# A decoder layer's prologue rearranged: bias copies, parameter rows, sample key products, low weight parts, the split of x

## The reference, cut to what matters

```
proj = x @ w_in                      # 3072 columns: conv gates and input, q, k, v
conv = B * conv3(C * h)              # 4 groups of 64 channels
attn = dilated window attention, 12 heads of 64, shared relative-position bias
       (prompt: 256 keys of its own; sample: 256 cached keys each, plus its own key)
x = LN(alpha*x + [conv, attn] @ w_out)
x = LN(alpha*x + memory attention (4 heads, 256 tokens))
x = LN(alpha*x + top-4-of-32 experts, clamped SwiGLU)
outputs also: new k and v rows, conv state, memory k and v
```

## Time and profile before

| | us |
|---|---|
| median of 3 executions | 1408.44 (1399.79 to 1411.55) |
| the profiled execution | 1414.02 |
| its span, first to last instruction | 1412.1 |
| TensorE busy | 1224.5 (87%) |
| VectorE busy | 376.2 (27%) |

### The profile page before, as it was taken

One profiled execution on the slowest core, in us unless ns is written; L12 is line 12 of the kernel. 1 busy time (PEld: TensorE's weight loads), 2 busy tenths in 40 slices (PEclk: granted clock), 3 DMA queues, 4 the chain that ended last, 5 costly groups with the idle time before them and its releaser, 6 DMA issues.

```text
span 1412.1 us, 16873 instructions
## 1 busy us (share of the span) xinstructions
PE 1224.5 (87%) x6509; PEld 617.4 (44%) x6509; DVE 376.2 (27%) x843; ACT 210.1 (15%) x370; POOL 78.8 (6%) x61
## 2 busy tenths in 40 slices
PE   3896997995887999999899998999889898898986
PEld 2894443874674334333433343333433333333332
DVE  3365433117325221202212032021220202212023
ACT  3441222022312010010110101101001010100001
POOL 2014300004001000000000000000000000000001
PEclk7998999998997999999999999999999999999999
DMA  9885799515991999999999999999999999999993
GB/s 289 178 255 164 181 164 337 179 65 201 364 417 74 364 418 416 416 419 417 419 418 416 417 419 417 419 417 416 418 419 418 419 417 416 418 418 418 417 416 130
DMA packets 104709, 487.17 MB, mean 345 GB/s; under 512 B 8948, under 2 KB 10636, under 8 KB 71296
## 3 DMA queue, kind: packets, MB, share of 16 engines
q1 hardware_dynamic: 99296, 469.47, 85.3%
q0 software_dynamic: 3824, 15.62, 4.2%
q10 hardware_dynamic: 1552, 1.57, 0.4%
HBM read 479.40 MB, written 7.24 MB: 345 GB/s over the span
## 4 chain that ended last, share of the span: by engine, by line
PE 56%; SPq 24%; DVE 9%; issue 4%; ACT 3%; DMA 3%; POOL 1%; DVEq 0%; POOLq 0%
PE ps L1730 19%; SPq L569 13%; SPq L565 11%; PE ps L1433 11%; PE ps L1752 10%; PE ps L1464 4%; PE ps L1762 3%; PE ps L1702 2%; DMA ring<-in_w_gate_up_dram 2%; PE ps L1583 1%; DVE arena L1350 1%; DVE ring L1064 1%; ACT arena L917 1%; PE ps L1418 1%; DMA arena<-in_b_gate_up_dram 1%
## 5 line engine op out<-in xcount | busy, mean ns | idle before, releaser
L1730 PE MATMUL ps<-ring,arena 128*64 128x512 f32 x1536 | 340.1, 594 | 11.7 <-DMA ring<-in_w_gate_up_dram 11.7
L1333 DVE TENSOR_SCALAR arena<-ps 128x512 f32<-128x512 f32 x32 | 22.2, 693 | 703.0 <-PE ps L1730 703.0
L1730 PEld LDWEIGHTS ps<-ring,arena 128*64 128x64 f32 x1536 | 108.8, 137 | 228.1 <-issue 188.4
L1752 PE MATMUL ps<-ring,arena 128*64 128x512 f32 x768 | 170.1, 596 | 22.6 <-ACT arena L917 22.6
L1762 PE MATMUL ps<-arena 128*128 128x264 f32 x256 | 92.4, 507 | 34.5 <-DVE arena L1350 33.6
L1752 PEld LDWEIGHTS ps<-ring,arena 128*64 128x64 f32 x768 | 53.1, 137 | 124.2 <-issue 95.9
L911 ACT ACTIVATE arena<-arena 128x512 f32<-128x512 f32 x32 | 20.2, 632 | 578.3 <-DVE arena L1333 578.3
L1433 PE MATMUL ps<-arena,ring 128*128 128x264 f32 x384 | 89.2, 395 | 5.1 <-DVE arena L1120 3.7
L1464 PE MATMUL ps<-x_split,w_split 128*128 128x264 f32 x576 | 75.0, 294 | 21.1 <-DVE w_split L949 21.1
L1762 PEld LDWEIGHTS ps<-arena 128*128 128x128 f32 x256 | 52.2, 239 | 80.5 <-DVE arena L1350 62.6
L1730 PE MATMUL ps<-late,arena 128*64 128x512 f32 x384 | 85.3, 593 | 0.3 <-DMA late<-in_w_gate_up_dram 0.3
(11 more groups left out here) (264 smaller groups left out, 990.6 us busy)
## 6 DMA issues: line engine op xcount, KB each, us to landing
ring<-in_w_gate_up_dram SPq DMA_DIRECT2D x192, 1024.0 KB, 20.5
ring<-in_w_down_dram SPq DMA_DIRECT2D x96, 1024.0 KB, 24.4
late<-in_w_gate_up_dram SPq DMA_DIRECT2D x48, 1024.0 KB, 19.3
late<-in_w_down_dram SPq DMA_DIRECT2D x24, 1024.0 KB, 23.4
arena<-in_w_gate_up_dram SPq DMA_DIRECT2D x16, 1024.0 KB, 19.2
ring<-in_w_in_dram SPq DMA_DIRECT2D x12, 1024.0 KB, 22.2
ring<-in_cache_mem_k_dram SPq DMA_DIRECT2D x8, 1024.0 KB, 4.9
ring<-in_cache_mem_v_dram SPq DMA_DIRECT2D x8, 1024.0 KB, 8.1
```

Of the source, the lines that this page charges most:

```text
L1333: nc.vector.tensor_scalar(g2, ps[:, 0, :], 7.0, None, ALU.min).then_inc(e_g2, 1)
L1730: ins = mm(ps[64 * j:64 * j + 64, gu, :], x, w[:, D * gu + 512 * j:D * gu + 512 * j + 512], start=(c < 0), stop=(c == 7), skip_group_check ...
L1752: ins = mm(ps[64 * j:64 * j + 64, 4 + half, :], x, w[:, kk, 512 * half:512 * half + 512], start=(m == 0), stop=(m == 7), skip_group_check= ...
```

## The change

- **Order of loads.** The memory tokens come behind the first four pieces of `w_in`.
- **x.** Each of the eight chunks gets a PSUM bank of its own. ScalarE only casts (`x_hi` from PSUM); VectorE copies `xT` from PSUM and subtracts `x_lo` from PSUM.
- **Low weight parts.** `w_lo` is written over the piece of `w_in` in the ring slot itself (`ring_split`, the same memory as float32r). So a slot is free when TensorE has used the piece, and no longer when VectorE has subtracted it; `w_lo` waits for no buffer.
- **Small work moved.** The bias matmuls and small turns (`small_turns`) run after `win_half(1)`, the memory's turns (`turn_memory`) after `win_half(3)`. The three casts of `b_gate_up` by ScalarE come after the first, second and third group of tiles (before: one ahead of the first weight piece, then after the first and second group). The convolution is spread over more pieces.
- **Parameters.** `w_conv` and the layer norms' scales and shifts are loaded as rows (38 rows of 512 B) and turned once by TensorE; before, 4-byte elements were loaded to columns.
- **Bias.** 16 copies of the row go to DRAM, and not 128; GpSimd reads the diagonals back with 16 DMAs (8 blocks of 16 partitions, two groups of heads) as soon as the copies have landed.
- **Token rows.** They use banks 4, 6, 0, 2, 4, 6; ScalarE copies three of the six, VectorE three. The sample's own scores (`own_scores`) move from ahead of the head loop into its step 1.
- **Sample key products.** VectorE makes them (`key_products`, in steps 2 to 9 ahead of `key_sums`); GpSimd only issues the four spread loads, and then the stores.

```diff
-    s = [("xp", 0), ("mp", 0)] + [("win", i) for i in range(12)]
+    s = [("xp", 0)] + [("win", i) for i in range(4)] + [("mp", 0)] + [("win", i) for i in range(4, 12)]
...
             elif what == "win":
-                eng.wait_ge(s_wlo, 2 * i + 2)
+                piece_used(eng, 2 * i + 1)
...
-            pool.dma_start(scratch_bias, b_row[0:H, :].unsqueeze(1).broadcast_to((H, P, 384))).then_inc(s_bscr, 16)
+            pool.dma_start(scratch_bias, b_row[0:H, :].unsqueeze(1).broadcast_to((H, SHIFTS, 384))).then_inc(
+                s_bscr, 16)
+            pool.wait_ge(s_bscr, 16)
+            for j in range(P // SHIFTS):
+                for i, (h0, h1) in enumerate(((0, SPLIT_HEADS), (SPLIT_HEADS, H))):
+                    diagonals = bass.AP(scratch_bias.tensor, P - 1 - SHIFTS * j + SHIFTS * 384 * h0,
+                                        [[383, SHIFTS], [SHIFTS * 384, h1 - h0], [1, 256]])
+                    pool.dma_start(bias_parts[i][SHIFTS * j:SHIFTS * j + SHIFTS], diagonals).then_inc(s_bias, 16)
...
-            for b in range(NS):
-                if b % 2 == 0:
-                    spread("qb", scratch_q, AW, b // 2, s_spread)
-                products("qb", "wk", AW, b)
+            for i in range(NS // 2):
+                spread("qb", scratch_q, AW, i, s_spread[i])
...
-                nc.scalar.copy(xT[:, c, :], ps[:, c % 4, 0:T]).then_inc(s_xT_out, 1)
-                act.wait_ge(s_xT_out, c + 1)
-                nc.scalar.copy(x_hi[c], xT[:, c, :]).then_inc(s_xhi, 1)
-            act.wait_ge(s_bgu, 48)
-            nc.scalar.copy(bgu3[0:2 * NX, :], bgu_f[0:2 * NX, :]).then_inc(s_bcut, 1)
+                nc.scalar.copy(x_hi[c], ps[:, c, 0:T]).then_inc(s_xhi, 1)
...
+                nc.vector.tensor_copy(xT[:, c, :], ps[:, c, 0:T]).then_inc(s_xT_out, 1)
+                nc.vector.tensor_tensor(x_lo[c], ps[:, c, 0:T], x_hi[c].bitcast(F32), ALU.subtract).then_inc(s_xlo, 1)
+            low_parts(0, 4)
             dve.wait_ge(s_bt, 1)
...
+            def key_products(b):
+                arrived(dve, ("qb", b // 2))
+                arrived(dve, ("wk", b))
+                q = slot(("qb", b // 2))[:, (b % 2) * AW:(b % 2 + 1) * AW]
+                k = halves(("wk", b))[:, :, 0:AW]
+                nc.vector.tensor_tensor(k, k, q.unsqueeze(1).broadcast_to((P, 2, AW)), ALU.mult).then_inc(s_kq, 1)
...
+                if step == 1:
+                    own_scores()
                 if 2 <= step < 2 + NS:
+                    key_products(step - 2)
                     key_sums("wk", AW, H, step - 2, step - 1, s_kr)
...
             for i in range(6):
                 win_half(i)
+                if i == 1:
+                    small_turns()
+                if i == 3:
+                    turn_memory()
```

More of the change, by code:

```diff
@@ L232, in decoder_layer, with bias_of @@
         pt = view(a_pt, 2, 512)
-        assert top[0] == ARENA + LATE
+        a_tail = region(3 * D)
+        assert top[0] == ARENA + LATE and a_tail <= ARENA + EARLY
+        bias_parts = (view(a_mix + 4 * T, SPLIT_HEADS, 256), view(ARENA + EARLY, H - SPLIT_HEADS, 256))
+        def bias_of(h):
+            return bias_parts[0][:, h, :] if h < SPLIT_HEADS else bias_parts[1][:, h - SPLIT_HEADS, :]
         x_hi, x_lo = ([x_split[:, i, c, :] for c in range(DC)] for i in range(2))
-        w_hi, w_lo = ([w_split[:, b, i, :] for b in range(2)] for i in range(2))
-        bgu_f = view(a_mix, 2 * D)
+        w_hi = [w_split[:, b, :] for b in range(2)]
+        bgu_f = view(a_proj + K0 * T, 2 * D)
         b_row = view(a_xh + D, 384)
[L239 to L242, removed]
+        es = view(a_tail, 264)
+        pts = view(a_tail + 264, 2, 128)
+        selfw = view(a_tail + 264 + 256, 128)
+        avs = view(a_tail + 264 + 384, 2, D)
         stT = tiny(2 * 16).rearrange("p (c n) -> p c n", c=2)
@@ L245, in decoder_layer @@
         ul = tiny(2 * 2).rearrange("p (c k) -> p c k", c=2)
-        wc = tiny(6).rearrange("p (k c) -> p k c", k=3)
-        gcol = [tiny(DC) for _ in range(2)]
-        bcol = [tiny(DC) for _ in range(2)]
+        par = tiny(6 + 4 * DC)
+        wc = par[:, 0:6].rearrange("p (k c) -> p k c", k=3)
+        gcol, bcol = ([par[:, 6 + DC * (2 * i + j):6 + DC * (2 * i + j) + DC] for i in range(2)] for j in range(2))
+        par_rows = view(a_xh + D + 384, P)
         mx, nm, sm, rs = (tiny(4).rearrange("p (a b) -> p a b", a=2) for _ in range(4))
@@ L295, in decoder_layer @@
         assert 804 + T <= 2 * AW
-        extra = [view(a, 2048) for a in (a_memT, a_memv, a_lg, a_bias + D)]
-        yo = view(a_bias, 3, D)
+        extra = [view(a, 2048) for a in (a_memT, a_memv, a_lg, a_tail + D)]
+        yo = view(a_tail, 3, D)
         landed = [sem(f"landed{s}") for s in range(RING)]
@@ L342, in decoder_layer @@
         s_yz = sem("s_yz")
-        s_spread = sem("s_spread")
+        s_spread = [sem(f"s_spread{i}") for i in range(4)]
         s_conv = sem("s_conv")
@@ L429, in arrived @@
                 if key[0] == "qb":
-                    eng.wait_ge(s_spread, 16 * (key[1] + 1))
+                    eng.wait_ge(s_spread[key[1]], 16)
                 else:
@@ L639, in _ @@
                                   tab[0:NX + 1, :].unsqueeze(1).broadcast_to((NX + 1, NS, H))).then_inc(s_zero, 1)
[L640 to L645, removed]
+            pool.dma_start(par_rows[0:6, :], w_conv[0].rearrange("k (c p) -> (k c) p", p=P)).then_inc(s_par, 16)
+            for i, v in enumerate((ln1_g, ln1_b, ln2_g, ln2_b)):
+                pool.dma_start(par_rows[6 + DC * i:6 + DC * i + DC, :], v[0].rearrange("(c p) -> c p", p=P)).then_inc(
+                    s_par, 16)
+            with nc.allow_non_contiguous_dma(reason="one router bias per row"):
                 pool.dma_start(brc[0:NX, :], b_router[0].rearrange("(e a) -> e a", a=1)).then_inc(s_par, 16)
@@ new lines, in small_turns @@
+            def small_turns():
+                pe.wait_ge(s_const, 48)
+                pe.wait_ge(s_zero, 2)
+                oh = con("oh")[0:NX + 1, :]
+                tb = tab[0:NX + 1, :]
+                mm(ps[0:H, 4, 0:384], tb, oh[:, 0:384], start=True, stop=True)
+                for c in range(2):
+                    mm(ps[:, 5, c * H:(c + 1) * H], oh[:, 384 + c * P:384 + (c + 1) * P], tb, start=True, stop=True)
+                mm(ps[0:NS * H, 5, 32:33], tab8[0:NX + 1, :], oh[:, 640:641], start=True, stop=True)
+                for c in range(2):
+                    tp(ps[:, 6, 16 * c:16 * c + 16], xh[0:2 * NS, 0, P * c:P * c + P], ident[0:2 * NS, 0:2 * NS])
+                pe.wait_ge(s_par, 16 * 6)
+                n_par = 6 + 4 * DC
+                tp(ps[:, 6, 32:32 + n_par], par_rows[0:n_par, :], ident[0:n_par, 0:n_par]).then_inc(s_bt, 1)
```

169 lines of the change are left out of this document (85 added, 84 removed).

## The result

The changed kernel takes 1413.73 us (median of 20 runs, 1407.55 to 1423.26), the kernel before 1405.93 (20 runs beside it, 1395.61 to 1412.57): ratio 1.0059, 95% interval 1.0037 to 1.0082. It is slower, by 0.6%, where I had forecast 1394 and 1380 to 1405. Its profiled execution took 1410.73, span 1408.9. That pair of profiles misleads: the one of before took 1414.0, 8 above the median of its kernel, the one of after 3 less than its median.

What follows compares the result with a forecast made beforehand. Bound by a prologue until the first expert frees slots, then a DMA-rate load stream. Terms -16.4, +1.6, -8.9, +3.1, +6 sum to -14.6 from profiled 1414.0: 1399.4; median 5.6 lower, so 1394, range 1380 to 1405.

Steps and rivals of the forecast that it cites:

- What goes through the DMA queues in the loop: Head loop: earlier GpSimd stores and later SyncE loads share the queues; TensorE waits some 6 us, range 0 to 14.
- rival B: Head loop: slow DMA stretch also catches step 5's load, landing 27 us after issue; 1403 to 1405 us, chance 0.12.
- Start of the w_in products: Prologue: first `w_in` product starts at 17.2 us instead of 33.67, -16.4 us.
- What moves into the products: During the `w_in` products: small and memory turns added there, some old waits gone; +1.6 us, range 0 to +6.
- The ring: Weight slots freed 3 to 6 us later; loads behind them needed after 100 us, so no cost before the head loop.
- Bias and parameters: Prologue DMA: smaller bias write and its reading back stay hidden, freed bandwidth is worth nothing; 0 us.
- End of the products to the first probabilities: Between `w_in` products and first head: shorter copies, own scores moved, faster scalings, less slow clock; -8.9 us, range -6 to -11.
- The head loop: Key products on VectorE lengthen three uncovered TensorE waits to 2.9 us; +3.1 us, up to 6 more by the clock.

Runs made afterwards that it cites:

- run 9: Changed kernel with key products and sums only in head-loop steps covered by a half of the memory products, element stores left in place: 1396.28 us, ratio 0.9935.
- run 10: Changed kernel with key products and sums only in covered head-loop steps, and the four element stores replaced in place by whole-row stores: 1381.60 us, ratio 0.983.
- run 12: Kernel before without the four element stores, that part of the output left out: 1407.91 us, ratio 1.001.
- run 5: Changed kernel without the four element stores, that part of the output left out: 1395.21 us, ratio 0.9926.
- run 7: Changed kernel with element stores moved behind the memory key store and ScalarE's first `b_gate_up` cast back ahead of the weights: 1410.30 us, ratio 1.0027.
- run 11: Changed kernel with element stores moved behind the memory key store and 128 shifted bias copies again instead of 16: 1399.07 us, ratio 0.9951.
- run 1: Changed kernel with the four element stores moved behind the memory key store, after the sample attention: 1401.59 us, ratio 0.9966.
- run 2: Changed kernel with all eight stores of that block, large ones too, moved behind the sample attention: 1401.90 us, ratio 0.9956.
- run 6: Changed kernel with element stores moved behind the memory key store, and key products and sums only in covered head-loop steps: 1388.91 us, ratio 0.9871.
- run 3: Kernel before with the four element stores moved behind the memory key store: 1404.88 us, ratio 0.9987.

## Why the prediction was wrong

The step that failed is *What goes through the DMA queues in the loop*. Its term was +6, within 0 to 14; in its place the runs show 18.5 us (the changed kernel with and without the element stores, 1413.7 and 1395.2), and 12.1 when they are only moved. I had the parties right: the elements, GpSimd's early arrival, SyncE's late loads, a rate of 10 to 50 GB/s. The order was wrong. I counted the last `w_mem_v` as queued ahead of the elements, arriving in time, and let only `w_mem_k` fall into the low stretch. Counted, as the prediction does, from the scores of step 3 (127.64 in the profile after), the load was to share the queues from +5; it was issued at +8.4, and the first element store at +6.9. My own rows gave the price of being caught: 26.9 us from issue to landing, measured now at 27.99. The wait is 16.72 us, and the half behind it runs in part at the lower clock (8.84 against 7.13). The half at 135.96 (9.22) stands ahead of that wait, behind the one of 2.97 for VectorE. That is the mechanism of rival B ("the hole takes both"), to which I gave 0.12 and the reason "the load is queued before the elements start"; that reason was false. Its time, 1403 to 1405, was some 9 us too low, because less had been won elsewhere than I summed, as the table below shows.

The Trainium skill's rule of turns between queues, packet by packet (DMA: Bandwidth & Descriptors, Queues, rings and completion order), would, with the even share of bytes that I read into it, have made this term about 0. The runs decide against the even share: runs 9 and 10 store the same bytes around the same load, and it lands after 25.9 us in one and 10.0 in the other. Whether the turns by packet hold, no run here shows. Another rule of the same page bears on that pair (Rules for kernel authors): a transfer whose last dimension isn't contiguous becomes one descriptor per element, and should be rearranged. The runs agree that it should be rearranged here, 14.7 us between the two.

The other steps, from the profiles of run 12 and run 5. Both leave out the element stores, so the low stretch that they cause is in neither. Each is a single execution, 2.7 and 4.3 us above its median. TensorE's first start of each stage, us:

| stage begins | run 12 (before) | run 5 (changed) | difference | forecast |
|---|---|---|---|---|
| first turn of probabilities | 132.6 | 110.7 | -21.9 | -23.7 |
| sample attention | 232.9 | 217.6 | -15.3 | -20.6 |
| `w_out` products | 247.3 | 236.8 | -10.5 | -20.6 |
| first layer norm | 279.4 | 268.9 | -10.5 | -20.6 |
| first gate and up products, streamed | 456.9 | 446.3 | -10.6 | -20.6 |

- *Start of the w_in products*, -16.4: right. 16.45 against the 17.2 said; run 7 showed that it passes to the end.
- *What moves into the products*, +1.6, and *The ring*, 0: right. The wait behind piece 3 is 2.13, `w_in` ends at 100 (101 said).
- *Bias and parameters*, 0: right for the bias copies (run 11); the parameters as rows were not run by themselves.
- *End of the products to the first probabilities*, -8.9: right within 1 to 2 us; with the two steps above -21.9 of -23.7.
- *The head loop*, +3.1 and up to +9: the mechanism is right, the term too small. The three waits are 2.97, 2.93 and 2.93, as said (2.9). The stage got longer by 6.6 in the table (run 5 against run 12): 3.0 are the waits for VectorE, 1.0 is a wait for `w_mem_v` that is left without the stores, and 2.5 are the same products taking longer (TensorE busy 92.7 us in place of 90.1), the clock, which I had let be the same in both.
- Not in the prediction at all: the sample attention. It takes 14.4 us in run 12 and 19.2 in run 5, with the same products and the same short waits ahead of them. The changed order alone doesn't bring this: runs 1 and 7, which have it, took 14.4 us, the changed kernel 16.0 and run 2 19.2. The first window of that stage, of run 12 and then of run 5, shows only another clock:

```profile
233.00:239.00 6.00, 6.00 (x64) 1.49 (x64) 0.00 (x0) 0.80 (x1) 0.00 (x0) 1.00 0.06 5
```

```profile
218.00:224.00 6.00, 6.00 (x40) 1.14 (x32) 0.00 (x0) 0.00 (x0) 0.00 (x0) 0.53 0.00 0
```

- The rest passes whole: -10.5 at `w_out`, -10.6 at the experts, and the medians differ by 1407.9 - 1395.2 = 12.7. That is 7.9 us less than the 20.6 forecast for these steps together; with the 12.5 us by which the 18.5 exceed the 6, it makes up the miss of 19.7.

So against before: 12.7 us won, 18.5 lost to the elements, 5.8 slower by this sum and 7.8 measured. The forecast had -20.6 and +6.

Not settled: what VectorE waits for where the trace names no releaser in its core (3.30 us in run 1; none in run 5, without the stores). Moved stores seem to cost something still in the changed order: run 5 is 6.4 us below run 1, and run 10 is 7.3 below run 6, but the intervals overlap in both pairs. And a single profile places such differences badly. From the first layer norm to the first expert the profiles took 168.5 (run 3), 168.6 (the changed kernel), 172.3 (run 5) and 181.3 us (run 2), at mean granted clocks of 0.93, 0.93, 0.91 and 0.87, while from the first expert to the end all fourteen profiles (before, after and the twelve runs) took 956.6 to 958.7.

## What to carry to other kernels

Taking work off an engine moves everything behind it in its list forward. Before such an edit, write down what is behind it (here eight stores, four of them of 2560 elements in all), and what other list is released at the same moment; then ask which load would be caught. What a store of elements costs depends on what stands beside it (nothing in the old order, 18.5 us in the new) and not on its few bytes: turn it into rows (two small transposes and a copy here; from the last `w_in` product to the first turn of probabilities run 10 takes 10.1 us and run 6 takes 9.7) wherever a load that somebody waits for can stand beside it, and only then take the gain of the earlier start. And a step of work that fits under a covering block is to be placed by that block, not by its turn: that alone was worth 12.7 us with the element stores moved (run 6 against 1) and 17.5 with them in place (run 9 against the changed kernel).

## What was not expected of the hardware

- 10 KB written as 4-byte elements hold the DMA engines at a share above 1 and 22 to 81 GB/s for about 12 us, and everything queued with them (a 1 MB load 25.2 to 28.0 us, a 0.4 KB write 22 to 25 us) lands after. The same bytes as 1 KB rows leave no such stretch: the load lands in 10.0 and the small write in 7.9.
- The granted clock differs between stages that the trace shows alike: the same products after the same waits of 1.3 and 0.7 us ran at 1.00 in run 12 and at 0.53 in run 5 (whole stage: 14.4 us in runs 1, 7 and 12, 19.2 in runs 2 and 5). TensorE was busy all through both windows (6.00 of 6 us), so neither a wait in the stage nor its neighbours in the trace tells which level comes; what does stays open. The mean granted clock was 0.954 over the 20 runs of the changed kernel and 0.960 over the 29 of before in the first group.
